# Keys and queries normed channel by channel in a streaming encoder, and key and value rows stored from SyncE's queue

## What is computed

```python
kvf = rmsnorm(x, kv_norm_g) @ w_kvf
k = rmsnorm(kvf[..., :B_WIDTH].reshape(bsz, seq, 16, 128), k_norm_g)   # per head
v = kvf[..., B_WIDTH:2 * B_WIDTH].reshape(bsz, seq, 16, 128)
q, z = split(rmsnorm(x, norm_g) @ w_in, 2)
q = rmsnorm(q.reshape(bsz, seq, 16, 128), q_norm_g)                    # per head
o = softmax(q k^T / sqrt(128) + f_q - f_k, causal) v
y = (o * silu(z)) @ w_out
```

## Time and profile before

| | us |
|---|---|
| median of three runs | 1642.24 (1639.4 to 1642.29) |
| the profiled execution | 1639.89 |
| its span from first to last instruction | 1637.9 |
| kv stage, chunk 0 of group 0 to chunk 15 of group 3 | about 1013 to 1239 |
| fox stage | about 1240 to 1638 |

### The profile page before, as it was taken

The page is one execution under the profiler, slowest core; times in us unless marked ns, Lnnn a source line. Parts: engine busy times, 40 slices in busy tenths (PEclk is TensorE's granted clock), DMA queues, the critical chain, the costliest instruction groups (busy, mean ns, idle before and its releaser), DMA issues.

```text
span 1637.9 us, 29229 instructions
## 1 busy us (share of the span) xinstructions
PE 1614.1 (99%) x11523; PEld 1546.4 (94%) x11523; DVE 1114.9 (68%) x2141; ACT 757.9 (46%) x1254; POOL 385.8 (24%) x710
## 2 busy tenths in 40 slices
PE   8999999999999999999999999999999999999997
PEld 7999999999989999999999989999999998999997
DVE  5876666766677867768687788676536546563855
ACT  5545344443554453535445445545333544535451
POOL 1210111011234232321322311044136603030004
PEclk9999999999999999999999999999999999999999
DMA  6576667656876676666756555466558855575535
GB/s 194 174 200 167 181 187 210 166 172 188 231 209 217 204 236 187 208 208 200 243 177 221 188 187 172 129 208 192 165 190 219 215 172 142 174 181 166 159 116 109
DMA packets 312727, 305.72 MB, mean 187 GB/s; under 512 B 75688, under 2 KB 292288, under 8 KB 312592
## 3 DMA queue, kind: packets, MB, share of 16 engines
q1 hardware_dynamic: 274784, 223.07, 47.2%
q0 software_dynamic: 29984, 79.12, 15.0%
q10 hardware_dynamic: 7824, 1.68, 0.6%
HBM read 259.49 MB, written 44.30 MB: 185 GB/s over the span
## 4 chain that ended last, share of the span: by engine, by line
PE 92%; DVE 4%; ACT 1%; issue 1%; DMA 1%; ACTq 0%; POOL 0%; DVEq 0%
PE acc L178 26%; PE acc L180 25%; PE acc L179 25%; PE aux L1516 3%; PE aux L1363 2%; PE aux L1489 2%; DVE w_lo L158 1%; PE aux L1342 1%; PE aux L2779 1%; PE aux L1523 1%; PE aux L1535 1%; PE aux L2835 0%; PE aux L1470 0%; PE aux L2802 0%; PE aux L2836 0%
## 5 line engine op out<-in xcount | busy, mean ns | idle before, releaser
L158 DVE TENSOR_TENSOR w_lo<-raw,w_hi 128x1024 fp32r<-128x1024 f32 x400 | 484.6, 1218 | 257.4 <-ACT w_hi L153 255.4
L153 ACT ACTIVATE w_hi<-raw 128x1024 fp32r<-128x1024 f32 x400 | 414.9, 1055 | 239.9 <-PE acc L180 226.7
L178 PE MATMUL acc<-xg_hi,w_hi 128*128 128x304 f32 x1536 | 470.8, 306 | 1.5 <-DVE w_lo L158 1.5
L180 PE MATMUL acc<-xg_hi,w_lo 128*128 128x304 f32 x1536 | 464.2, 302 | 0.0
L179 PE MATMUL acc<-xg_lo,w_hi 128*128 128x304 f32 x1536 | 462.9, 301 | 0.0
L105 POOL TENSOR_TENSOR cell<-cell 1x1 f32<-1x1 f32 x148 | 77.1, 521 | 1000.8 <-DVE xc_lo L904 318.8
L178 PEld LDWEIGHTS acc<-xg_hi,w_hi 128*128 128x128 f32 x1536 | 289.7, 189 | 5.6 <-issue 3.1
L179 PEld LDWEIGHTS acc<-xg_lo,w_hi 128*128 128x128 f32 x1536 | 290.4, 189 | 0.8
L180 PEld LDWEIGHTS acc<-xg_hi,w_lo 128*128 128x128 f32 x1536 | 289.8, 189 | 0.0
L178 PE MATMUL acc<-xb_hi,w_hi 128*128 128x288 f32 x512 | 155.7, 304 | 2.9 <-DVE w_lo L158 2.8
L178 PE MATMUL acc<-hz_hi,w_hi 128*128 128x304 f32 x512 | 155.1, 303 | 0.4 <-DVE zs L988 0.4
(11 more groups left out here) (487 smaller groups left out, 2977.4 us busy)
## 6 DMA issues: line engine op xcount, KB each, us to landing
raw<-in_a_w_in SPq DMA_DIRECT2D x128, 512.0 KB, 3.9
raw<-in_a_w_out SPq DMA_DIRECT2D x64, 512.0 KB, 4.3
raw<-in_w_kvf SPq DMA_DIRECT2D x64, 512.0 KB, 4.5
raw<-in_b_w_in SPq DMA_DIRECT2D x64, 512.0 KB, 4.6
raw<-in_b_w_out SPq DMA_DIRECT2D x32, 512.0 KB, 3.6
raw<-in_a_wq SPq DMA_DIRECT2D x16, 512.0 KB, 4.0
raw<-in_a_wk SPq DMA_DIRECT2D x16, 512.0 KB, 4.2
raw<-in_a_wv SPq DMA_DIRECT2D x16, 512.0 KB, 5.3
```

Source lines behind the costliest of these rows:

```text
L153: act.activation(w_hi[:, s, :, :], raw[:, s, :, :], ACT.Copy).then_inc(hi_made, 1)
L158: dve.tensor_tensor(w_lo[:, s, :, :], raw[:, s, :, :], w_hi[:, s, :, :].bitcast(F32), ALU.subtract).then_inc(lo_made, 1)
L178: pe.matmul(acc[b][:, 0:width], wh, x_hi[:, k0 + k, :], start=st, stop=False)
L180: mm = pe.matmul(acc[b][:, 0:width], wl, x_hi[:, k0 + k, :], start=False, stop=last and k == 3)
```

## The change

Both norms stay channel-major. ACT takes each result twice from PSUM, once copied and once squared; PE sums the squares over the channels with four matmuls against columns of ones, 32 columns wide, each into its own 32 partitions; DVE multiplies by the squared token factor over 128 (`rs2`), adds the epsilon, and makes the inverse root over 128 partitions x 304 (or 288) tokens. ACT sends the four rows to DRAM and, when they have landed, brings them back spread over all partitions (`kR`, `qR`), both on its own DMA queue. DVE makes the finished keys or queries with four operations. Key rows are now turned by DVE in blocks like the values. All block stores, 24 for keys and 24 for values of a group, are issued by SP, six behind each weight load of j = 4 to 11 of the next group.

```diff
-        def store(eng, g, name, src, done):
...
-        def store_values(eng, g, done):
+        def store_rows(eng, g, name, blk, done, quarters=range(4)):
+            wait(eng, blk_made, g.times(2) + (BLK_V + (2 if name == "v" else 1)))
+            for a in quarters:
...
+        def rows_beside(sp, g, j):
+            if 4 <= j < 8:
+                store_rows(sp, g, "k", key_blk, k_out, (j - 4,))
+            if 8 <= j < 12:
+                store_rows(sp, g, "v", val_blk, v_out, (j - 8,))
...
                 for n, j, _ in steps(g):
                     kv_chunk_load(sp, n, g, j)
+                    rows_beside(sp, g + -1, j)
...
-            gk_load(Count(0))
+            for s, name in enumerate(("k_norm_g", "q_norm_g")):
+                src = i[name] if s == 0 else i[name][0]
+                for k in range(BH):
+                    pool.dma_start(g_qk[:, s, k:k + 1], src[k].rearrange("(p a) -> p a", a=1)).then_inc(g_landed, 16)
...
-                store(pool, g, "k", k_t, k_out)
...
+                    act.activation(kf[:, d, :], acc[u.turn(4)][:, 0:T], ACT.Copy)
+                    ins = act.activation(k_sq[:, d, :], acc[u.turn(4)][:, 0:T], ACT.Square)
...
+            def rows_out(g):
+                wait(act, k_norm, g.times(2) + 2)
+                act.dma_start(kr_dram[g.value], kn[0:P:32, 2, :]).then_inc(k_rows, 16)
+            def rows_back(g):
+                wait(act, k_rows, g.times(32) + 16)
+                wait(act, k_final, g)
+                act.dma_start(kR[:, :, :], kr_dram[g.value].unsqueeze(0).to_broadcast([P, GRP, T])).then_inc(k_rows, 16)
...
+                    if j == 11:
                         inverse_norms(g)
+                    if j == 13:
+                        rows_out(g)
+                    if j == 14:
+                        rows_back(g)
...
+            def norm_terms(g):
+                wait(dve, t_ready, g + 1)
+                dve.tensor_tensor(kn[:, 0, :], aux[0][:, 0:T], rs2[:, :], ALU.mult).then_inc(t_free, 1)
+                dve.tensor_scalar(kn[:, 0, :], kn[:, 0, :], EPS, None, ALU.add).then_inc(k_norm, 1)
+            def key_rows(g):
+                wait(dve, k_root, g + 1)
+                inverse_root(dve, own, kn[:, 2, :], kn[:, 1, :], kn[:, 0, :], kn[:, 3, :])
+                dve.tensor_tensor(kn[:, 2, :], kn[:, 2, :], rstd_row[:, :], ALU.mult).then_inc(k_norm, 1)
+            def keys_final(g):
+                wait(dve, k_rows, (g + 1).times(32))
+                for m in range(GRP):
+                    ins = dve.scalar_tensor_tensor(kb[:, m, :], kf[:, m, :], g_qk[...], kR[:, m, :], ALU.mult, ALU.mult)
+                ins.then_inc(k_final, 1)
+            def key_blocks(g):
+                wait(dve, k_final, g + 1)
+                blocks_of(key_blk, kb, k_out, g)
...
+                    if j == 0 and not first:
+                        key_blocks(g + -1)
                     if j == 1 and not first:
                         value_blocks(g + -1, tile)
+                    if j == 10:
                         norm_terms(g)
+                    if j == 12:
+                        key_rows(g)
                     if j == 15:
-                        keys_back(g)
+                        keys_final(g)
...
-        QUERIES = {0: "q", 1: "r n K0 K1", 2: "f K2 K3", 3: "s", 4: "b"}
+        QUERIES = {0: "q K0", 1: "r n K1", 2: "f", 3: "A s K2", 4: "B K3", 5: "b"}
+        ATTEND_1 = {**ATTEND, 5: "b X0 Y"}
+        BESIDE = {0: {**QUERIES, **ATTEND_1}, 1: {**QUERIES, **ATTEND_1, 16: "q", 17: "r n", 18: "f", 19: "A", 20: "B s", 22: "b"},
+                  2: {1: "K0 K1", 2: "K2 K3", **ATTEND, 16: "q", 17: "r n", 18: "f", 19: "A", 20: "B s", 22: "b"},
...
+        Y_EARLY = (((0, (0, 1)),), ((1, (0, 1)), (2, (0, 1))), ((3, (0, 1)), (0, (2,)), (1, (2,)), (2, (2,)), (3, (2,))))
+        Y_LATE = (((0, (0, 1, 2)), (1, (0, 1, 2)), (2, (2,)), (3, (2,))), ((2, (0, 1)), (3, (0, 1))), ())
+        Y_LAST = (((0, (0, 1, 2)), (1, (0, 1, 2))), ((2, (0, 1, 2)), (3, (0, 1, 2))), ())
+        Y_PARTS = [Y_EARLY] * 5 + [Y_LATE] * 2 + [Y_LAST]
...
             for n, kind, g, j, _, _ in order[SLOTS:]:
                 fox_load(sp, n, kind, g, j)
+                if g == 0 and kind != "OUT":
+                    rows_beside(sp, Count(GROUPS - 1), j if kind == "Q" else j + 8)
...
+            def q_sums(g):
+                for x in range(GRP):
+                    r = 32 * x
+                    mm = pe.matmul(bank[r:r + 32, 0:TQ], ones[:, 0:32], q_sq[:, x, :], start=True, stop=True,
+                                   tile_position=(0, r))
...
```

More of the change, by code:

```diff
@@ L1816, in fox_load @@
                 load_chunk(sp, n, i["b_w_in"][0, 512 * (j % 4):512 * (j % 4 + 1), col:col + CW])
-        t_free = [sem(f"t_free{b}") for b in range(3)]
+        t_free = sem("t_free")
         def head_parts(ap, n):
@@ L1886, in keys_out @@
             def keys_out(g):
-                wait(pool, k_final, (g + 1).times(3))
-                settled(own, cell[:, :])
-                store(pool, g, "k", k_t, k_out)
-                for b in range(3):
-                    wait(pool, t_free[b], g.times(2) + 2)
+                wait(pool, k_final, g + 1)
                 settled(own, cell[:, :])
@@ L2013, in take_values @@
+            def key_blocks(g):
+                wait(dve, k_final, g + 1)
+                blocks_of(key_blk, kb, k_out, g)
+            counted["key blocks"] = key_blocks
             def take_values(n, j, tile):
@@ L2055, in turn @@
                         norm_1()
-                    if first and j == 9:
-                        columns()
                     if first and j == 10:
@@ L2425, in fox_gpsimd @@
                 kc_load(g)
-                for t in range(3):
-                    freed(pool, use(g - 1, "b", t))
-                settled(own, cell[:, :])
-                gq_load(g)
                 pool.wait_ge(use_ready, use(g - 1, "X3") + 1)
@@ L2561, in q_terms @@
             def q_terms(g):
-                for t in range(3):
-                    dve.wait_ge(q_squared, 3 * g + t + 1)
-                    own.done(dve.tensor_reduce(qst[:, 0, GRP * t:GRP * (t + 1)], head_parts(q_sq[:, t, :], P),
-                                               AX.X, ALU.add))
-                own.wait()
-                dve.tensor_scalar(qst[:, 1, :], qst[:, 0, :], 1.0 / P, EPS, ALU.mult, ALU.add).then_inc(q_var, 1)
+                written(dve, use(g, "q"))
+                if g:
+                    dve.wait_ge(q_rows, 32 * g)
+                u = use(g, "q")
+                dve.tensor_tensor(qn[:, 0, :], aux[u % 4][:, 0:TQ], rs2[:, META:T], ALU.mult).then_inc(use_free[u % 4], 1)
+                freed(dve, u)
+                dve.tensor_scalar(qn[:, 0, :], qn[:, 0, :], EPS, None, ALU.add).then_inc(q_norm, 1)
             def turn_keys(g, x):
@@ L2723, in fox_vector @@
                         counted["value blocks"](Count(GROUPS - 1), Count(A_FOX))
+                    if j == 0:
+                        counted["key blocks"](Count(GROUPS - 1))
                     if j == 4:
@@ L2772, in scores @@
                     pe.wait_ge(F_low, 1)
-                    for t in range(3):
-                        freed(pe, use(g, "b", t))
+                    pe.wait_ge(q_final, g + 1)
                 bank = free_bank(use(g, f"X{x}"))
@@ L2790, in scores_new @@
                         r = x * DEC
-                        pe.matmul(bank[r:r + DEC, 0:keys.shape[-1]], q_new2[:, x, :], keys[:, x, :],
+                        pe.matmul(bank[r:r + DEC, 0:keys.shape[-1]], qT[:, x, 256:TQ], keys[:, x, :],
                                   start=True, stop=False, tile_position=(0, r))
@@ L2870, in fox_tensor @@
                 if (kind, g, j) == ("Q", 0, 7):
[L2872 to L2873 removed]
+                    pe.wait_ge(t_free, GROUPS)
                     pe.wait_ge(lf_taken, 1)
```

327 lines of the change are left out of this document (111 added, 216 removed).

## The result

The changed kernel takes 1643.16 us (median of 20 runs, 1641.29 to 1648.92) against 1640.62 for the kernel before (20 runs, 1639.4 to 1642.29): ratio 1.0018, 95% interval 1.0012 to 1.0024. That is 0.18% slower, clear of noise but under the 0.2% that I had counted as a change. I had forecast 1635 and faster; the range holds the time, the forecast and its direction were wrong. The profiled execution took 1642.07, 2.2 us more than the one before (1639.89), where my sum gave 6.7 less. So 8.9 us are to be found.

The account below looks back on a forecast made before the run. PE, busy 99% of the span, was taken to bound the kernel: 1639.9 - 23.1 (PE's account) + 5.9 (SP's queue) + 9.5 (first queries) + 1.0 (end) = 1633.2 us, said as 1635 for the median; range 1618 to 1648.

Parts of the forecast that it names:

- PE's own work: On PE, 16 groups of transposes at 1.31 and `rcol` leave, -22.3 us; eight groups of sums at 0.56 come, +4.5.
- The period of SP: On SP's queue, one load and six stores take 3.47 us, more than a chunk, so a late start stays late.
- Q0 and Z0: First chunks of the fox stage: loads behind SP's stores come late from chunk 5 on, PE waits 3.2 us.
- late splits of the kv stage: In the kv groups, PE waits for late splits: none in group 1, 1.1 us in group 2, 1.6 in group 3.
- K: When a group's blocks are ready for SP's stores, counted from PE's end of chunk 15: 5.7, 7.3 and 7.9 us.
- The root on DVE: The inverse root over 304 tokens on DVE, about 4.5 us, counted in the chains to the rows.
- The first queries: At X0, PE waits for root, rows out, rows back and products: 8.2 us, second group 1.3, sum 9.5.
- The end: Last y stores: SP's last issue ends later than POOL's did, + 1.1, taken as 1.0 us.
- The offset: Median of the runs lies 2.35 us above the profiled execution; with part of it, 1633.2 becomes 1635.
- One: Rival: SP's queue keeps up, no group is late, first queries wait about 1.3 us each: 1620; chance 0.27.
- Two: Rival: stores cost more than 0.49 us on SP's queue, slower from 0.55 on, 1656 at 0.6; chance 0.16.
- Three: Rival: PE's sums of squares don't overlap, four take 2.25 us, 13.5 more, 1648; chance 0.04.

Follow-up runs that it names:

- experiments 1: The changed kernel with SP's block stores two loads later, behind j = 6 to 13 instead of 4 to 11: 1640.66 us, ratio 0.9998 to the kernel before.
- 6: The changed kernel with stores two loads later and the cached keys of group 0 loaded paced instead of 16 DMAs in a row: 1637.37 us, ratio 0.9983.
- Experiment 4: The changed kernel with stores two loads later, the first queries' factor and root one chunk earlier, and OUT events in a chunk each: 1632.05 us, ratio 0.9944.
- experiment 9: The changed kernel with stores two loads later, query events moved, value loads behind query rows, cached keys paced, last group's value stores three loads later: 1622.97 us.
- (2): The changed kernel with four stores behind each load of j = 4 to 15 in place of six over 4 to 11: 1634.0 us, ratio 0.9958.

## Why the prediction was wrong

**PE's own work: right but for the sums.** All 16 groups of transposes gave 1.31 each as forecast. Four sums cost 0.81 to 0.85, not 0.56: I took the pace inside a run of 16, where the entry to it and the first matmul behind it count little, and the change makes eight short runs. This is 2.1 us of the miss.

**The period of SP: the step that failed first.** "In the mix stage four periods of one load and six stores take 13.87 us, 3.47 each", taken for the kv and the fox stage. It measured 3.99, 3.59 and 3.66 in the kv groups and 3.91 in Q0 and Z0. The late splits of the kv stage came to 6.8 instead of 2.7, the largest part of the miss. In group 1 the start was as forecast, and seven periods took 27.95 instead of 24.3; I had chunk 5 usable 1.05 before PE wants it, and PE lost 2.7 where I had 0. In group 2 the blocks were ready at K = 7.7 (forecast 7.3), but one issue of 1.64 stands among the first six stores, and chunk 5's load came 1.5 later than my sum has it. Group 3 came out smaller than forecast, 1.1 for 1.6, since its K was 5.9 and not 7.9: there two errors cancel. The 3.47 is right for most periods; what it lacks are the rare long issues, six of the seven with an instruction packet at the same time. That such an issue waits for that packet is not shown: no run moved either. That a stretched issue can also come from other traffic on the DMA engines is shown for the cached keys (experiments 1 and 6). For `kT_scratch` in group 1 it is only likely. In Q0 and Z0 the agreement, 3.7 for 3.2, is partly luck: the load of chunk 5 was issued at 1247.73, 9.3 after PE began the stage at 1238.45, where K + 3.05 gave 10.95, and the seven periods then took 3.1 more than mine.

**The root on DVE: a step that was missing.** I used the root's 4.5 us in the chains to the rows and nowhere else. It is also 4.3 us in which DVE makes no split, where the split's lead is less. This costs 1.4 each in OUT0 and OUT1: 2.8 us. At chunk 5 of Z0 it holds PE up by 2.1 too, but that is no loss of its own: the scores wait for the chain that begins with this root, and PE would have stood 2.1 longer there. My line that the splits "keep a lead of several us" was about ACT; for DVE I never checked it. Experiment 4 took the two waits in OUT away by position alone.

**The first queries: the chain right, the price not.** The two stops of PE beside this chain, 2.1 and 6.3, make 8.4 for my 8.2, and the second group 1.6 for 1.3; late splits, the root and the rows' trip in series. What I put at nothing is the clock: PE stood idle and was granted half of it for the scores, 2.8 us more. So the 8.8 that the place costs is near my 8.2 by luck, 6.3 of wait and 2.5 of clock. What I also missed is that the trip depends on what else moves: rows out took 1.6, 3.2, 4.0 and 6.0 in four of the kernels. My 2.3 for this leg was too small and 5.7 for the other too large.

**The end: wrong sign.** I compared issue times of two queues and left out what comes behind them (and 1630.0 + 4.4 is 1.4 behind 1632.98, not 1.1): POOL's drain of 3.4 us, which the kernel before had at its very end and the change has not. 2.7 the other way.

**The offset.** I put 1.8 us between the profiled execution and the median, from three runs before (2.35). By 20 runs it was 0.7, and after the change 1.1. This is outside the 8.9 and made the forecast look 0.7 nearer.

**The rivals.** One, "the queue keeps up", did not happen as the change places the stores. Its cost argument was the sentence of the Trainium skill, page "DMA: Bandwidth & Descriptors", section "Issuing engines are not separate DMA queues", that initiating a DMA is usually small beside the DMA itself. That compares one issue with its own DMA, mostly 0.4 to 0.5 us here beside 2 to 4 to landing, and no run contradicts it; I had held it against a chunk. What counts for this queue is that six issues took 3.0 to 4.6 where a chunk takes 3.34. But it can be made to happen, by starting later (experiments 1 and 9) or by four stores a load (2): experiment 9, with four more edits, is at 1623, near the 1620 of that rival. Two, "stores dearer on this queue", was the right mechanism at a smaller size: in group 1 a period was 0.5 longer, 0.09 for each of six stores, in groups 2 and 3 0.02 and 0.03, against the 0.06 above 0.49 that I said would bring the run to slower by 0.2%. I had it decide at once on all 192 stores; in fact a few single issues are long and the rest are not, and PE pays only what exceeds its lead. Three, "sums don't overlap", was wrong: 0.81 to 0.85, not 2.25.

In sum, 8.9 us: kv splits 4.1, root before splits in OUT 2.8, the clock at the first scores 2.8, sums 2.1, PE's stops on the way to the first and second queries 0.5, Q0 0.5, old waits and the start of the stage -0.6, the end -2.7, and -0.6 that I can't place.

## What to carry to other kernels

Before work is moved onto a queue that also carries the weights, write down when the first of it can start and compare the period with the consumer's beside every other transfer of the new place, not in the place where it was measured, and over a stretch long enough to hold what comes only once in 15 to 20 us; if the period is longer than a step, a late start is never made up, and starting later or issuing fewer per step is better than the same bunch early. A long operation on the engine that feeds the bound one costs nothing only if the feed's lead at that step exceeds it: ask this at each place in the order, not once for its total. A stop of several us on TensorE may cost more than its length, by the clock granted behind it. And after one wait is removed, look at what the early work now collides with: here a load that had been late before met the critical row trip.

## What the runs showed that I had not expected

- The time SP needs to issue a DMA is not fixed. Four stores took 1.98 in quiet stretches, 3.27 beside the store of `kT_scratch`, 3.57 with an instruction packet of 16 KB among them, and 6.64 beside POOL's 16 loads of cached keys.
- After waits of 3.1 to 12.8 us at the first scores PE was granted 0.50 of the clock for part or all of them, after 2.1 us it was not. In the change this cost 2.8 us beside a wait of 6.3.
- From the last issue to the end of the span 1.4 us passed with SP last and 4.9 with POOL last, for stores of the same y. POOL's drain of 3.4 to 4.7 us makes the difference, and it costs nothing when POOL is done early.
- Four rows of 288 tokens took 1.6 to 6.0 us to DRAM, and 4.8 to 10.6 to come back spread over 128 partitions, by what else was under way.
- Moving loads of 1.6 MB off the way of 4.5 KB gave 5.7 us.
